# Where the small products of the mixers stand in TensorE's order: behind a whole GATE or BRANCH unit, or in its middle

## The reference

```python
h = rmsnorm(x, p['norm1_g']) * (1 + sc1) + sh1
u, q, k, v, z, xbc, dt_raw = split_sizes(h @ p['w_in'], IN_SIZES)
o_pool = multiscale_pool_mixer(u, p['pool_w'], p['pool_scale'])
...
o_att = diff_attention(q, k_keys, v_keys, lam)
o_att = (rmsnorm(o_att, p['att_subln_g']) * (1 - lam_init)).reshape(b, n, ATT_DIM)
o_ssd, h_f, h_b = ssd_mixer(z, xbc, dt_raw, p, h0[0], h0[1])
gate_pool, gate_att, gate_ssd = jnp.split(jax.nn.sigmoid(h @ p['w_gate'] + p['b_gate']), 3, axis=-1)
merged = gate_pool * (o_pool @ wb_pool) + gate_att * (o_att @ wb_att) + gate_ssd * (o_ssd @ wb_ssd)
x = x + g1 * (merged @ p['w_out'])
h2 = rmsnorm(x, p['norm2_g']) * (1 + sc2) + sh2
up = dwconv_centred(h2 @ p['ffn_w_up'], p['ffn_conv_w'], p['ffn_conv_b'])
a_gate, a_val = jnp.split(up, 2, axis=-1)
x = x + g2 * ((jax.nn.silu(a_gate) * a_val) @ p['ffn_w_down'])
```

## Time and profile before

| | us |
|---|---|
| median of 3 runs | 1328.78 |
| lowest, highest | 1327.65, 1329.33 |
| the profiled execution's own time | 1328.28 |
| its span, first to last instruction | 1326.5 |
| PE busy in it | 1296.1 (98%) |
| DVE busy | 1086.6 (82%) |
| ACT busy | 652.9 (49%) |
| stretch of the slots 0 to 33, layer 0 and layer 1 | 192.9 and 192.8 |

### The profile page before, as it was taken

One profiled execution on the slowest core, in us unless ns is written; L12 is line 12 of the kernel. 1 busy time (PEld: TensorE's weight loads), 2 busy tenths in 40 slices (PEclk: granted clock), 3 DMA queues, 4 the chain that ended last, 5 costly groups with the idle time before them and its releaser, 6 DMA issues.

```text
span 1326.5 us, 20238 instructions
## 1 busy us (share of the span) xinstructions
PE 1296.1 (98%) x7634; PEld 1242.6 (94%) x7634; DVE 1086.6 (82%) x2038; ACT 652.9 (49%) x1058; POOL 164.9 (12%) x158
## 2 busy tenths in 40 slices
PE   7999999999999999999999999999999999999997
PEld 5999889998999999999999988899999899999997
DVE  6899888678887989899968998877878889999533
ACT  5643555644556454543375335546455654545332
POOL 0076000001220000000103900000032000000010
PEclk9999999999999999999999999999999999999999
DMA  9566345333352444457735562553235344444441
GB/s 363 190 222 231 120 154 193 122 104 112 117 184 94 147 159 143 162 178 265 239 112 191 200 205 77 187 191 106 86 122 195 96 143 144 160 143 155 143 125 54
DMA packets 58641, 210.00 MB, mean 158 GB/s; under 512 B 6704, under 2 KB 9136, under 8 KB 57008
## 3 DMA queue, kind: packets, MB, share of 16 engines
q1 hardware_dynamic: 56512, 199.71, 45.1%
q0 software_dynamic: 2032, 9.00, 2.1%
HBM read 205.01 MB, written 3.67 MB: 157 GB/s over the span
## 4 chain that ended last, share of the span: by engine, by line
PE 75%; DVE 14%; ACT 6%; issue 3%; DMA 1%; SPq 1%; DVEq 0%; ACTq 0%; POOLq 0%
PE acc L967 22%; PE acc L968 22%; PE acc L969 22%; DVE wl L1719 2%; DVE gates L1944 1%; DVE cv L1900 1%; DVE junk_late L1808 1%; PE mix L1127 1%; DVE ee L2030 1%; DMA head<-in_whead_dram 1%; PE mix L1222 1%; ACT wh L1310 1%; PE mix L1155 1%; DVE hl L1724 1%; ACT hh L1335 1%
## 5 line engine op out<-in xcount | busy, mean ns | idle before, releaser
L967 PE MATMUL acc<-hh,wh 128*128 128x384 f32 x1519 | 517.8, 341 | 1.3 <-DVE hl L1724 0.7
L969 PE MATMUL acc<-hh,wl 128*128 128x384 f32 x1519 | 507.9, 334 | 0.0
L968 PE MATMUL acc<-hl,wh 128*128 128x384 f32 x1519 | 507.7, 334 | 0.0
L1719 DVE TENSOR_TENSOR wl<-raw,wh 128x1024 fp32r<-128x1024 f32 (+1 forms) x276 | 341.4, 1238 | 69.7 <-ACT wh L1310 68.6
L1310 ACT ACTIVATE wh<-raw 128x1024 fp32r<-128x1024 f32 (+1 forms) x276 | 287.0, 1041 | 135.8 <-PE acc L969 135.5
L967 PEld LDWEIGHTS acc<-hh,wh 128*128 128x128 f32 x1519 | 285.1, 188 | 13.8 <-issue 8.0
L968 PEld LDWEIGHTS acc<-hl,wh 128*128 128x128 f32 x1519 | 285.2, 188 | 2.4
L969 PEld LDWEIGHTS acc<-hh,wl 128*128 128x128 f32 x1519 | 285.1, 188 | 0.0
L1900 DVE SCALAR_TENSOR_TENSOR cv<-acc,prm,cv 128x1 f32<-128x1 f32 (+1 forms) x416 | 153.7, 411 | 9.2 <-ACT cv L1473 1.9
L969 PE MATMUL acc<-ah,wl 128*128 128x384 f32 x352 | 117.6, 334 | 0.0
L967 PE MATMUL acc<-ah,wh 128*128 128x384 f32 x352 | 117.6, 334 | 0.0
(11 more groups left out here) (302 smaller groups left out, 1709.1 us busy)
## 6 DMA issues: line engine op xcount, KB each, us to landing
raw<-in_wstream_dram SPq DMA_DIRECT2D x248, 512.0 KB, 3.6
rawm<-in_wstream_dram SPq DMA_DIRECT2D x80, 512.0 KB, 4.3
raw<-in_wstream_dram SPq DMA_DIRECT2D x32, 448.0 KB, 3.4
head<-in_whead_dram SPq DMA_DIRECT2D x8, 1024.0 KB, 15.8
crow_late<-in_cvec_rows_dram POOLq DMA_DIRECT2D x2, 1024.0 KB, 6.6
crow<-in_cvec_rows_dram POOLq DMA_DIRECT2D x2, 1024.0 KB, 5.3
out_y_dram<-yt SPq DMA_DIRECT2D x3, 384.0 KB, 2.4
x<-in_xs_dram SPq DMA_DIRECT2D x1, 1024.0 KB, 7.6
```

Source lines behind the costliest of these rows:

```text
L967: mm(out, sh, mhi, start=start, stop=False)
L968: mm(out, sh, mlo, start=False, stop=False)
L969: return mm(out, sl, mhi, start=False, stop=stop)
L1719: tt(wl[:, s, 0:n], raw[:, raw_slot(u), 0:n], wh[:, s, 0:n].bitcast(F32), ALU.subtract).then_inc(lo_done, 1)
```

## The change

`unit` takes a third argument, `midway`: the number of a slot, or None. Unit 25 + s now issues the products of slot s in its own middle: a BRANCH unit between its two groups, behind the raise of `branch_half`, any other unit behind 4 of its 8 triples. The call behind the unit is gone. Each slot's products thus stand half a unit later than before, among the products of the next unit. The other engines' orders are untouched.

```diff
-            def unit(l, u):
+            def unit(l, u, midway):
                 kind, j, part = UNITS[u]
...
                         if jj == 0:
                             last.then_inc(branch_half, 1)
+                            if midway is not None:
+                                mixers(l, midway)
...
                     for k in range(KT):
+                        if k == KT // 2 and midway is not None:
+                            mixers(l, midway)
                         if first is not None:
...
                     elif u not in (1, 2, UP0 + 1, UP0 + 2):
-                        unit(l, u)
-                    if MIX0 <= u <= MIX0 + SLOT_RMS + 1:
-                        mixers(l, u - MIX0)
+                        unit(l, u, u - 1 - MIX0 if MIX0 < u <= MIX0 + SLOT_RMS + 2 else None)
```

## The result

The changed kernel takes 1342.46 us, the median of 5 runs (1340.88 to 1344.28), against 1329.33 us of the kernel before in the same session: a ratio of 1.0103 with a 95% interval of 1.0091 to 1.0115, +13.1 us. The forecast was 1338.7 us (1332.5 to 1344.0), slower.

A forecast was written before the change was run, and what follows sets the result against it. PE, 98% busy, bounds the kernel. 2.65 + 0.4 - 0.95 + 2.0 = 4.1 us a layer, 8.2 in all, plus 1.7 for the clock: 1338.2 us from the profiled execution, 1338.7 as median (1332.5 to 1344.0).

The forecast's parts named there:

- PE's waits are all that counts: Whole kernel: PE is busy for 98% of the span, so a new order can gain only PE's waits.
- slots that feed slots cost nothing: Slots whose results return through DVE and ACT to another slot keep their spacing on PE: cost nothing.
- The seam at BRANCH unit 0: Slot 27 no longer covers the pooling output's split ahead of BRANCH unit 0: +2.6 to +2.7 us a layer.
- T + 8.7 to T + 11.8: T is slot 25's start; PE ready for BRANCH unit 0 at T + 8.7, following its operand at T + 11.8.
- The backlog: DVE idles 2.7 us behind the first splits, so BRANCH unit 4 waits for group 4's bank: +0.4 us a layer.
- Slot 32: Its wait for ACT's square, behind DVE's last `gate_z`, goes: -0.95 us a layer (0 to -0.95).
- The seam at BRANCH unit 8: Less PE work behind slot 33 while DVE norms, then evicts group 12; wait 2.7 us for 0.65: +2.0 us a layer.
- The clock: PE's clock halves for 3.4 us behind long waits; one fall counted for the four new waits: +1.7 us in all.
- The rival in which the clock falls at each wait: The clock falls at all four new waits, +6.8 us, total 1343.8 us; chance 15%.

The follow-up runs named there:

- slots 0 to 26 alone: Kernel before with only slots 0 to 26 moved into the middle of the next unit, slots 27 to 33 behind whole units: 1329.24 us, ratio 1.0002.
- the filled waits: Idle products put in PE's waits: changed kernel's two seams, 1338.95 us; norms of the kernel before, 1329.23 and 1327.57; norms with three edits, 1325.57 and 1325.60.

## Why the prediction was right

**PE's waits are all that counts, and slots that feed slots cost nothing.** Shown by slots 0 to 26 alone: 1.0002. One such chain did come short, slot 25 to slot 27 in that run (1.10 us).

**The seam at BRANCH unit 0, +2.65 us a layer.** The wait was put at 3.1 us, T + 8.7 to T + 11.8; the starts are 3.14 us apart, 0.17 of which is the usual distance, so PE lost 2.97 us where it had lost 0.4: +2.55. That ACT's and DVE's chains end there together is shown by the changed kernel's rows and by the run with ACT's split first.

**The backlog, +0.4.** It is 0.6 us (0.75 less the usual 0.17), and DVE's gap behind the four `hl` is 2.83 us for the 2.7 forecast:

```profile
305.52 0.73 DVE L2057 SCALAR_TENSOR_TENSOR cv<-xbc,prm,mix 128x128 f32<-128x128 f32 x2 [2.83 <-PE mix L1226]
```

**Slot 32, -0.95.** The wait went as forecast, but it had never been that long. The 4.83 us from unit to slot already contain the 0.39 us that the row shows; the prediction adds it a second time. It was worth 0.6 us. With the backlog this makes about 0 where the sum had -0.55.

**The seam at BRANCH unit 8, +2.0.** 2.85 us between the starts against 0.77 before, +2.1. The bank of group 12 as its releaser is shown by the run in which DVE evicts first.

**The clock, +1.7.** Right as a mechanism, too small. The sum took one fall for the four new waits and 1.7 us for a fall. The runs show 13 us more at the lower level than before's, three to four falls; at 0.33 to 0.36 us for each that makes 4 to 5 us, and what the waits leave of the 13.1 us is 3.6. The number of falls was too low, the price of one too high on average: it is 1.5 to 1.6 us behind BRANCH unit 0, 0.7 behind BRANCH unit 8 (in all four such falls seen), 0.6 to 1.2 behind a norm. That is what is left of about 1.5 us lost at once: behind BRANCH unit 8 of layer 1 the changed kernel first fell back 1.6 us and had 0.9 of it again at the start of OUT, where the kernel before waits 0.46 us and the changed one does not. Not all the falls are at the new waits: one of the three extra falls of the profiled execution is behind a norm, a place that the prediction left unchanged. Waits 8.2 + clock 1.7 were forecast; measured are 9.5 + 3.6. Both errors point the same way, and the range held them.

**The rival in which the clock falls at each wait** has a part of the truth: in the profiled execution it fell behind two of the four new waits, and behind two of three norms. The Trainium skill (TensorE: Matmul & The Clock Gate, HAM oscillation — how this bites in real kernels) describes a kernel that loses its clock at every one of its waits, which are of 3 to 5 us. The prediction carried that over to waits of 2.7 to 3.1 us, for which the page does not say it; the waits here, of 2.15 to 2.8 us, lost the clock at 27 of 46 places. Whether it falls differs from wait to wait and from run to run, and with it the time of one kernel, which spreads over 6 us. That idle time is what brings it down is shown by the filled waits (0 of 16).

## What to carry to other kernels

On an engine that is 98% busy, small work between large units is also cover: before moving it, look for the seams where the next unit's operand is still being made, and compare that operand's chain with what stands in the shadow. Where two engines' chains end at one seam, find the later one first; where a PSUM bank is late, look at what its reader does before it. PE waits of 2 us and more can cost a second time through the clock (here 3.6 us on 9.5 us of waits), so a span that differs by a microsecond or two from run to run should be read with the granted clock beside it.

## What the hardware showed that was not expected

Products that compute nothing, in a wait of PE, made a kernel 3.5 us faster (0.26%). Two things stay open. Filled waits of 2.15 us at the norms kept the clock up in every profiled execution and still gave nothing that could be measured on the kernel before. And with three waits of under 1 us taken away, the time at the lower clock was 16 us a run in place of 10, behind norms whose own waits had not changed.
